# A two-layer hybrid decoder step: first loads split over three issuers, indexer pages by two, output projection as split products

## What is computed

```python
for l in range(DEPTH):
    h = rmsnorm(x, norm_mix[l])
    a, b, c, d = layer_inputs(h, w_in[l], lbs[l], pos)      # one combined projection
    # A: indexer scores sum_h w relu(iq . ik), top 256 keys, attention over them
    #    (sample group: indexer keys, K and V gathered through page_table)
    # B: HGRN2 recurrence; C: dilated window attention; D: retention
    mix = concatenate([o_a, hgrn_out(o_b), o_c, retention_out(o_d)])
    x = x + mix @ w_out[l]                                  # output projection
    h = rmsnorm(x, norm_ffn[l])
    x = x + (silu(h @ w_gate[l]) * (h @ w_up[l])) @ w_down[l]
y = rmsnorm(x, norm_final)
```

## Time and profile before

| | us |
|---|---|
| median of 3 runs | 3923.39 |
| lowest and highest | 3922.53, 3926.75 |
| profiled execution: its time | 3925.18 |
| profiled execution: its span | 3923.5 |
| TensorE busy | 3422.3 (87%) |
| VectorE busy | 1788.0 (46%) |
| ScalarE busy | 493.7 (13%) |

### The profile page before, as it was taken

How to read it: one execution, slowest core, us unless ns; L and a number is a source line. 1 busy time by engine, 2 the same in 40 slices (tenths; PEclk the granted TensorE clock), 3 DMA queues, 4 the chain that set the end, 5 groups by cost and what they waited for, 6 DMA issues and landing times.

```text
span 3923.5 us, 53714 instructions
## 1 busy us (share of the span) xinstructions
PE 3422.3 (87%) x20896; PEld 2833.8 (72%) x20912; DVE 1788.0 (46%) x3332; ACT 493.7 (13%) x966; POOL 243.4 (6%) x455
## 2 busy tenths in 40 slices
PE   4689989875698999999977998988758899999996
PEld 2457757753468999999954684767435699999996
DVE  2279962752415333333324998255531533333334
ACT  1200112131101000000012001132301100000001
POOL 0000041000000000000000003300000000000000
PEclk8889999778799999999989999996878999999998
DMA  5121144013111111111132114420230011111111
GB/s 189 45 74 38 58 149 142 7 58 142 51 38 38 40 48 42 45 45 53 33 105 64 54 33 130 127 76 13 99 138 22 27 52 47 44 43 44 46 46 61
DMA packets 123592, 255.56 MB, mean 65 GB/s; under 512 B 21405, under 2 KB 81694, under 8 KB 121550
## 3 DMA queue, kind: packets, MB, share of 16 engines
q0 software_dynamic: 37680, 126.94, 10.1%
q1 hardware_dynamic: 83150, 116.32, 8.5%
q10 hardware_dynamic: 2496, 8.65, 0.6%
HBM read 220.76 MB, written 35.60 MB: 65 GB/s over the span
## 4 chain that ended last, share of the span: by engine, by line
PE 75%; SPq 7%; DVE 6%; issue 5%; DMA 3%; ACT 1%; POOLq 1%; DVEq 1%; POOL 0%; ACTq 0%
PE PS L1040 13%; PE PS L1041 13%; PE PS L1042 13%; PE PS L609 10%; PE PS L893 6%; SPq L381 4%; PE PS L615 3%; PE PS L952 2%; SPq L376 2%; PE PS L669 2%; PE PS L734 2%; PE PS L708 2%; PE PS L689 1%; PE PS L728 1%; PE PS L1019 1%
## 5 line engine op out<-in xcount | busy, mean ns | idle before, releaser
L1040 PE MATMUL PS<-HNHR,WHR 128*128 128x352 f32 x2112 | 684.1, 324 | 26.6 <-DVE HnR L1501 22.3
L1041 PE MATMUL PS<-HnR,WHR 128*128 128x352 f32 x2112 | 678.5, 321 | 0.0
L1042 PE MATMUL PS<-HNHR,WSR 128*128 128x352 f32 x2112 | 677.5, 321 | 0.0
L609 PE MATMUL PS<-Hn,WS 128*128 128x352 f32 x1536 | 466.2, 467 | 51.1 <-DMA WS<-wjobs 45.4
L1571 DVE TENSOR_SCALAR_CACHE_REDUCE U<-U,smu 128x384 bf16<-128x384 f32 (+6 forms) x448 | 484.3, 1145 | 6.9 <-issue 0.9
L609 PEld LDWEIGHTS PS<-Hn,WS 128*128 128x128 f32 x1536 | 296.7, 194 | 219.9 <-DMA WS<-wjobs 47.5
L1040 PEld LDWEIGHTS PS<-HNHR,WHR 128*128 128x128 f32 x2112 | 397.3, 188 | 30.4 <-issue 21.2
L1041 PEld LDWEIGHTS PS<-HnR,WHR 128*128 128x128 f32 x2112 | 398.0, 188 | 0.0
L1042 PEld LDWEIGHTS PS<-HNHR,WSR 128*128 128x128 f32 x2112 | 396.8, 188 | 0.0
L1040 PE MATMUL PS<-HDHR,WHR 128*128 128x352 f32 x1056 | 346.0, 328 | 17.5 <-DVE HDLR L1501 17.5
L1041 PE MATMUL PS<-HDLR,WHR 128*128 128x352 f32 x1056 | 343.3, 325 | 0.0
(11 more groups left out here) (237 smaller groups left out, 3800.3 us busy)
## 6 DMA issues: line engine op xcount, KB each, us to landing
WS<-wjobs POOLq DMA_DIRECT2D x160, 512.0 KB, 3.9
WS<-wjobs POOLq DMA_DIRECT2D x48, 384.0 KB, 3.3
U<-ckT SPq DMA_DIRECT2D x16, 896.0 KB, 7.0
U<-cv SPq DMA_DIRECT2D x16, 896.0 KB, 6.3
U<-kT_pool SPq DMA_DIRECT2D x160, 64.0 KB, 1.9
xres<-U SPq DMA_DIRECT2D x2, 4224.0 KB, 13.5
U<-xres SPq DMA_DIRECT2D x2, 4224.0 KB, 13.1
U<-ikT SPq DMA_DIRECT2D x256, 32.0 KB, 2.0
```

Source lines behind the costliest of these rows:

```text
L609: i = mm(PS[:, base + c, 0:CW], w[:, k, :], Hn[:, k, c * CW:(c + 1) * CW], start=k == 0, stop=k == KR - 1)
L1040: mm(out, wh, xh, start=k == 0, stop=False)
L1041: mm(out, wh, xl, start=False, stop=False)
L1042: i = mm(out, wl, xh, start=False, stop=k == n - 1)
```

## The change

Five things, all in the text of the engines' programs:

1. First loads. SyncE loads the page table and x in four parts (two blocks each, semaphores x_ld0 to x_ld3) and goes on to pages. ScalarE issues the seven others (init_in). ScalarE's squares wait for the part of x that they read.
2. Bias tables. The strided part of bdil and the own-token columns are made by eight small copies on VectorE; ScalarE then issues 7 DMAs, btile last, after it has formed the first inverse.
3. Pages. SyncE issues indexer pages of sequences 0 to 3, GpSimd those of 4 to 7, between weight jobs 3 and 4. The store of x stands behind sequences 0 and 1.
4. Weights. GpSimd loads jobs 0 to 3 of layer one in its prologue, after the page table, and at a layer's end jobs 0 to 3 of the next layer as the slots come free. After layer two these read padding of zeros.
5. Output projection in split products. Eight halves of the mix (split_mix) and eight of the weights (split_out) are made by VectorE; TensorE waits for g_inv instead of g_mix, and in its first unit for each half of the mix (mx_split). Some offsets in U move, the sample group's values of D are loaded later, and ScalarE waits for the state stores ahead of its squares.

The diff, cut to its core:

```diff
@@ gpsimd
-            pool.wait_ge(line_out, 16)
-            pool.dma_start(btile, bass.AP(bline.tensor, 1155, [[LINE, 8], [-1, P], [1, SEQ]])).then_inc(tile_tab, 16)
+            pool.wait_ge(ptab_in, 16)
+            for j in range(NSLOT):
+                pool.dma_start(slot(j, job_floats(j)), wjobs[j, :, 0:job_floats(j)]).then_inc(w_in[j], 16)
...
+                def index_keys(n):
+                    if n == 7:
+                        pool.wait_ge(nrm_done, 6)
+                        pool.wait_ge(x_out, 16)
+                    pages(pool, L, ikT, IKB[n % NIK], iq_in[n], n, 64)
...
-                for j in range(NJOBS):
+                for j in range(NSLOT, NJOBS):
+                    if j == NSLOT:
+                        for n in range(4, NB):
+                            index_keys(n)
...
                 for i in range(NSLOT):
-                    pool.wait_ge(w_in[i], L * SLOT_SUM[i] + SLOT_SUM[i])
+                    load(NJOBS + i, job_floats(i), max(j for j in range(NJOBS) if j % NSLOT == i))
@@ sync
+            sp.dma_start(PT[:, :], ptab).then_inc(ptab_in, 16)
+            for i in range(4):
+                sp.dma_start(X[:, 2 * i:2 * i + 2, :], xT[:, 2 * i:2 * i + 2, :]).then_inc(x_ld[i], 16)
+            sp.wait_ge(ptab_in, 16)
...
-                sp.dma_start(xres, X).then_inc(x_out, 16)
-                for n in (0, 1, 2, 4, 5, 6, 3, 7):
-                    if n == 3:
+                for n in range(4):
+                    if n == 2:
+                        for i in range(4):
+                            sp.wait_ge(x_ld[i], 16)
+                        sp.dma_start(xres, X).then_inc(x_out, 16)
+                    elif n == 3:
                         sp.wait_ge(nrm_done, 6)
                         sp.wait_ge(x_out, 16)
-                    pages(sp, L, ikT, IKB[n % NIK], ik_in[n], n, n // NIK * 64)
+                    pages(sp, L, ikT, IKB[n], ik_in[n], n)
@@ tensor
-                pe.wait_ge(g_mix, 2)
+                pe.wait_ge(g_inv, 2)
                 for m in range(KR):
-                    loaded(pe, L, J_OUT + m)
+                    pe.wait_ge(wo_split, m + 1)
+                    hi, lo = out_hi(m), WSR[:, (J_OUT + m) % NSLOT, 0:1024]
...
                         for k in range(KR):
-                            i = mm(PS[:, u % 6, 0:CW], w[:, k, :], mixall[:, k, c * CW:(c + 1) * CW],
-                                   start=k == 0, stop=k == KR - 1)
+                            if u == 0:
+                                pe.wait_ge(mx_split, k + 1)
+                            w = slice(k * P, (k + 1) * P)
+                            mm(PS[:, u % 6, 0:CW], hi[:, w], mix_hi(k)[:, t], start=k == 0, stop=False)
+                            mm(PS[:, u % 6, 0:CW], hi[:, w], HNHR[:, k, t], start=False, stop=False)
+                            i = mm(PS[:, u % 6, 0:CW], lo[:, w], mix_hi(k)[:, t], start=False, stop=k == KR - 1)
@@ scalar, prologue
+            for t, a in ((U[0:32, INIT:INIT + LINE], onehot), (U[0:8, INIT + LINE:INIT + 2 * LINE], linemask),
+                         (U[0:32, INIT + 2 * LINE:INIT + 2 * LINE + 8], relb), (CT[:, :], consts), (GN[:, :], gains),
+                         (LBL[:, :, :], lblog), (BITU[:, :], bits_u)):
+                act.dma_start(t, a).then_inc(init_in, 16)
+            act.wait_ge(init_in, 7 * 16)
...
-            norm_squares(2, lambda n: None)
+            norm_squares(2, lambda n: act.wait_ge(x_ld[(n - 1) // 3 // 2], 16))
@@ vector
+            def split_out(L, m):
+                j = J_OUT + m
+                loaded(v, L, j)
+                if m >= NSLOT:
+                    v.wait_ge(wo_ps, 3 * (m - NSLOT + 1))
+                halve(out_hi(m), WSR[:, j % NSLOT, 0:1024], slot(j, 1024)).then_inc(wo_split, 1)
+            def split_mix(k):
+                halve(mix_hi(k), HNHR[:, k, :], mixall[:, k, :]).then_inc(mx_split, 1)
```

More of the change, by code:

```diff
@@ L173, in build @@
         init_in = ctx.enter_context(nc.semaphore("init_in"))
+        ptab_in = ctx.enter_context(nc.semaphore("ptab_in"))
+        x_ld = [ctx.enter_context(nc.semaphore(f"x_ld{i}")) for i in range(4)]
+        iq_in = {n: ctx.enter_context(nc.semaphore(f"iq_in{n}")) for n in range(4, NB)}
         line_ps = ctx.enter_context(nc.semaphore("line_ps"))
@@ L204, in build @@
         iqz0, iqz = sem("iqz0"), sem("iqz")
-        ik_in = [sem(f"ik_in{i}") for i in range(NB)]
+        ik_in = [sem(f"ik_in{i}") for i in range(4)]
         ss_ps, ss_relu, ss_wsel, ss_sum, ss_done = map(sem, ("ss_ps", "ss_relu", "ss_wsel", "ss_sum", "ss_done"))
@@ L578, in _ @@
             mm = pe.matmul
-            pe.wait_ge(init_in, 9 * 16)
+            pe.wait_ge(init_in, 7 * 16)
             for q in range(5):
@@ L1182, in _ @@
             norm_inverse(2)
+            act.wait_ge(line_sb, 13)
+            act.dma_start(bline, U[0:8, LSUM:LSUM + LINE]).then_inc(line_out, 16)
+            act.dma_start(bdil[:, :, 0:384], U[4:8, LDIL:LDIL + NT * 384].rearrange("h (t j) -> h t j", t=NT)
+                          ).then_inc(line_tab, 16)
+            own = U[0:8, LOWN:LOWN + NT * NS].rearrange("h (t j) -> h t j", t=NT)
+            act.dma_start(bsamp[:, :, PAST:SW], own).then_inc(line_tab, 16)
+            act.dma_start(bdil[:, :, CK:CW_KEYS], own[4:8]).then_inc(line_tab, 16)
+            act.wait_ge(line_out, 16)
+            line, o = bline.tensor, 4 * LINE + 3
+            act.dma_start(bsamp[:, :, 0:PAST], bass.AP(line, 3, [[LINE, 8], [-1, NT], [1, PAST]])).then_inc(line_tab, 16)
+            act.dma_start(bdil[:, :, 384:CK], bass.AP(line, o + 1536, [[LINE, H], [-1, NT], [1, 512]])
+                          ).then_inc(line_tab, 16)
+            act.dma_start(btile, bass.AP(line, 1155, [[LINE, 8], [-1, P], [1, SEQ]])).then_inc(tile_tab, 16)
             def project(nos):
@@ L1468, in _ @@
             v.memset(EPSC, EPS)
-            v.wait_ge(init_in, 9 * 16)
+            v.wait_ge(init_in, 7 * 16)
             v.tensor_copy(idb[:, :], ident)
@@ L1865, in gla_d, with finish_d @@
                 i.then_inc(g_sat, 1)
-            def finish_d():
+            def finish_d(L):
                 z1 = Hn[:, 2:4, :]
+                v.wait_ge(g_in, 2)
+                for k in range(4, 6):
+                    split_mix(k)
                 v.wait_ge(g_mean, 2)
@@ L1873, in finish_d @@
                 i.then_inc(g_cen, 1)
+                for m in range(4):
+                    split_out(L, m)
                 v.wait_ge(g_inv, 2)
@@ L1878, in finish_d @@
                 tt(out=mixd, in0=mixd, in1=dr[:, 4:6, :], op=ALU.mult).then_inc(g_mix, 1)
+                v.drain()
+                for k in range(6, 8):
+                    split_mix(k)
             def split_weights(L, f, i, n):
@@ L1941, in _ @@
                 gla_d()
+                for k in range(4):
+                    split_mix(k)
                 states(1)
-                finish_d()
+                finish_d(L)
                 add_out(L)
@@ L2055, in _layout @@
     f = np.float32
-    W = np.zeros((DEPTH, NJOBS, P, SLOT), f)
+    padded = np.zeros((DEPTH * NJOBS + NSLOT, P, SLOT), f)
+    W = padded[0:DEPTH * NJOBS].reshape(DEPTH, NJOBS, P, SLOT)
     w_in = inp["w_in"].reshape(DEPTH, KR, P, -1)
@@ L2091, in _layout @@
     return {
-        "xT": xT, "wjobs": W.reshape(DEPTH * NJOBS, P, SLOT), "gains": gains, "consts": ct, "bits_u": bits,
+        "xT": xT, "wjobs": padded, "gains": gains, "consts": ct, "bits_u": bits,
         "ropet": rope, "decays": decays, "onehot": onehot, "linemask": line, "relb": inp["rel_bias"], "lblog": lbl,
```

98 lines of the change are left out of this document (45 added, 53 removed).

## The result

The kernel before took 3922.96 us (median of 4 runs, 3916.42 to 3926.75), the changed one **3821.72 us** (4 runs, 3818.35 to 3834.18). The ratio is **0.9741**, 95% interval 0.9723 to 0.9758. The forecast was 3791 us with a range of 3779 to 3818: the direction was right, the gain is 101 us in place of 132, and the time lies 3.7 us above the range.

The account below looks back on a forecast made before the run. TensorE's own instructions and its waits for indexer pages and weights were taken as the bound; gains 18.2 + 43.5 + 12.8 + 15.6 + 42.0 = 132.1 us, from 3923.4, gave 3791 us, range 3779 to 3818.

Parts of the forecast that it names:

- Output projection: Both layers: split products at 0.1605 us each replace float32 ones at 0.606; gain 21.0 us per layer, 42 in two.
- Rival (b): Output projection does not shorten because TensorE waits for VectorE's halves in every row; 3833 us, chance 0.04.
- (c): Slower than before: TensorE's clock stays at 1.2 GHz through the output projection; 3957 us, chance 0.02.
- Pages: Sample-group scores: no waits for indexer keys once two engines issue them; gains 43.5 us in layer one, 15.6 in layer two.
- Rival (a): Pages gain nothing: transfers, not issues, set their end, or GpSimd is as late as SyncE was; 3850 us, chance 0.05.
- Start: Program start: first projection begins at 44.2 us instead of 62.44; gain 18.2 us, bounds 9 and 21.
- constants at 15 us: Program start: three queues share evenly, so constants take 12.5 us plus some 2.5 us of issue and landing.
- My poor bound: Program start: loads share badly, constants land at 24 us, and the gain there is only 9 us.
- rival (d): Program start: constants land with everything else at 24 us; 3800 us, inside the range, no separate chance given.
- Start of layer two: Weights loaded at the end of layer one let TensorE start at 1991.4 us instead of 2004.22; gain 12.8 us.
- its drain is waited for by SyncE, but the issues (0.5 us each) are over before ScalarE's inverse is, so they cost nothing: Layer end: GpSimd's four added weight-load issues finish before ScalarE's inverse, so they add no time.
- the poor ends of the terms together: Whole kernel: lowest gains of all five terms (9, 35, 11, 8, 34) at once give 3826 us.

Follow-up runs that it names:

- drain_first: Changed kernel with GpSimd signalling its layer's end before issuing the next layer's four weight loads, not behind them; 3813.15 us, ratio 0.9719.
- ordered_start: Changed kernel with GpSimd's end-of-layer signal before the four weight loads, and first loads in sequence: constants, x, weights; 3794.61 us, ratio 0.9677.
- unchanged program: The changed kernel run once more with no edit; 3816.41 us, ratio 0.9737, profiled span 3810.7 us.

## Why the prediction came out as it did

**Output projection: right.** The forecast of 21.0 us per layer is 22.3 from the ready inverse to the last addition, less 1.3 for an inverse that comes later. The first was measured at 22.0 and 22.3. The second was 0.4 in layer one (41.8 us from the first split, where L1710 had stood, to the inverse, 41.4 before), and in layer two that stretch was not longer at all (41.8 against 44.4). Every step of the placing was seen: splits on VectorE in its idle stretches, TensorE's early start with six halves, two stops. They were 1.3 and 1.2 us where one of about 3 was forecast, and the first unit of 24 products ended 9.8 us after the inverse. Rival (b), a wait in every row, and (c), a clock that stays low, are excluded by the window at 0.98 with 89.00 us busy of 89. What the term left out is behind it: the norm sums that took 1.7 us more in each layer.

**Pages: right in both layers.** 43.2 against 43.5 and 15.5 against 15.6 in the execution with the full clock. What I had not seen is that the two edits overlap in layer one. Nor is the value of the split in layer two the 15.6 us: without it the wait would have grown, since TensorE's first projection comes earlier against SyncE's pages, and 28.2 us would have been lost. The fourth group came at 157.4 us in layer one, not at 148: TensorE was 8.9 us later from the start on. Rival (a) is excluded.

**Start: the step "constants at 15 us" failed.** 9.4 us were gained, not 18.2. I took the group of 1.5 MB to be through when three times its bytes have moved. Its bytes nearly were: 1.54 MB by 14 us. What the step left out is that the last three of the seven loads are many small packets, and that the three queues got packets, not bytes, in equal number: the last 0.04 MB, 438 packets, waited their turn beside the larger packets of x, pages and weights until 25.3 us. So 15 us was the time of the large constants and not of the group. My poor bound had 24 us (rival (d), the constants land with everything else). It met the time, but by luck: the first part of x had landed at 8.3 us, and of the constants only the small loads were late. That fewer competitors make the group earlier is shown by experiment: 25.3 us beside x, pages and weights, 20.9 without what GpSimd issues, 9.6 alone. That the small packets are what was late is read from the queues' rows; no run gives the same bytes in fewer packets. The other steps held and gave 1.5 us back: 25.5 us from constants to Hn (24.6 and 2.6 forecast; the eight copies took 1.5 us), 2.2 us to the first product.

**Start of layer two and end of the program: the step "its drain is waited for by SyncE, but the issues (0.5 us each) are over before ScalarE's inverse is, so they cost nothing" failed.** I counted the four issues and not the drain behind them. The issues were indeed over at 1926.9, before ScalarE at 1933.0. But the drain has 8.3 us of its own, 10.8 there, and it moved from a place where it was covered to behind TensorE's last products. The price is 4.6 us between the layers and 4.7 us at the end of the program, which the forecast didn't look at. In the drain_first and ordered_start traces it is gone but for 0.7 us between the layers of the latter.

**Sum.** Against the forecast the unchanged program in its second trace missed 19.3 us: 8.8 at the start, 5.2 at the start of layer two (4.6 of it the drain's), 4.7 at the end, 0.4 in the pages, and 2.5 us net of changes elsewhere (with the 3.4 us of the norm sums behind the output projection among them), less 2.3 us that the projection's own stretches gave more than the 42.0. That is 3810.7 where I had 3791.4. Ordered_start undoes the first causes and has a span of 3788.8. The range was too narrow as well: the poor ends of the terms together gave 3826, and I cut it at 3818 because not all of them would come. One did come, and the drain's two costs, which were in no term, came with it. The median missed by 31 us: these 19.3, and most of the rest is the 9 us between the median (3821.7) and the time of the execution with the full clock (3812.4).

**What stays open.** The median of the changed kernel is 3821.7 and 3816.4 in two comparisons, 4 to 9 us above an execution of 3812.4 with the full clock in the prompt scores. In three of the seven traces of the changed kernel and its variants whose prompt scores are unedited (the profiled execution, drain before loads, weights after constants) the clock fell in one layer's scores, at a cost of 19.3, 13.1 and 7.6 us; in the other four, in before and in before with split pages it didn't. All have the same instructions there and nearly the same load of TensorE: 26.7 us busy of 31 in the changed kernel's window at 1.00, 27.1 in that of the kernel before. What decides it from one execution to the next the runs don't tell. With two traces of before and its variant, whether the change made it more frequent is open too.

## What to carry to other kernels

When an engine's last act in a loop is moved behind a new wait, price everything that stands behind it in its queue, also what no list of waits and no chain ever shows: look up the instruction's own duration in the trace of before. Count a load in packets as well as in bytes: beside two other full queues 438 small packets, 0.04 MB in all, took 11 us here, and the 1.54 MB ahead of them 14. What is wanted first came first here only when a wait kept the other loads out of flight, whatever engine issued them. And gains that share a resource are not additive: the page split in layer two protected the earlier start, and in layer one it did what freeing a queue had done already. A faster stretch can also slow what stands behind it, as the norm sums show.

## What the runs showed of the hardware

- GpSimd's drain took 8.31 us in every execution with nothing issued just before, and 10.4 to 11.2 us behind four loads (five traces each); ScalarE's drain at the same place took 2.48 us (in the kernel before and in the changed one).
- A group of first loads of 1.58 MB in 688 packets landed at 25.3, 20.9 or 9.6 us, by what else was in flight. From 15 to 21 us, with three queues full, 212, 211 and 211 packets of them moved, with 1.66, 0.80 and 0.02 MB.
- The same 40 products of 64 rows (80 records) took 29.75 us at a granted clock of 1.00 and 49.0 us at a mean of 0.56, in different executions of one program.
- Six records of norm sums behind a pause of TensorE of 2.6 us took 2.04 us at a granted clock of 1.00 behind float32 products and 3.73 us at 0.55 behind the split ones.
- In the output projection TensorE began at a pitch of 0.29 us, came to 0.18 and 0.16 us around its second stop (1037.3 to 1039.5 us), fell back to 0.29, and was at 0.16 us from 1042.9 us on, 13 us after it had begun.
